# Latent attention rebuilt, the norm between two models folded in, and another order in a softmax loop

## The reference

```
return rms_norm(h, g_final)                         # end of the first model, x of the second

cq, ckv, kr = split(x @ w_in, [384, 640])           # latent attention
q = heads(rms_norm(cq, q_norm) @ w_uq)              # 16 heads, 64 plain + 32 rotary columns
kv = heads(rms_norm(ckv, kv_norm) @ w_ukv)          # 64 key + 64 value columns each
logits = (qn @ kn.T + rotary(qr) @ rotary(kr).T) * 96 ** -0.5
p = softmax(where(kpos <= qpos, logits, -1e30))
out = from_heads(p @ v) @ w_o
```

## Time and profile before

| what | value |
|---|---|
| median of three runs | 2787.2 us |
| the profiled execution | 2785.38 us, span 2783.6 us |
| mean granted clock of TensorE | 0.975 |
| PE busy | 2654.8 us (95%) |
| VectorE busy | 1745.5 us (63%) |
| ScalarE busy | 1342.4 us (48%) |
| HBM read | 452.38 MB, 163 GB/s over the span |

### The profile page before, as it was taken

One profiled execution on the slowest core, in us unless ns is written; L12 is line 12 of the kernel. 1 busy time (PEld: TensorE's weight loads), 2 busy tenths in 40 slices (PEclk: granted clock), 3 DMA queues, 4 the chain that ended last, 5 costly groups with the idle time before them and its releaser, 6 DMA issues.

```text
span 2783.6 us, 38348 instructions
## 1 busy us (share of the span) xinstructions
PE 2654.8 (95%) x14970; PEld 2271.9 (82%) x14970; DVE 1745.5 (63%) x1901; ACT 1342.4 (48%) x1554; POOL 6.8 (0%) x17
## 2 busy tenths in 40 slices
PE   7899998999899999999999999999789999999998
PEld 7688786887788988888887888887668888888887
DVE  6666676666666656666666666666536666666665
ACT  5444454444544545454444544544435454454543
POOL 0000000000000000000000000000000000000000
PEclk9899997999999999999999999999879999999999
DMA  7255442554455335555533455554305555543452
GB/s 281 76 184 182 174 167 76 184 182 173 158 187 194 139 106 201 191 176 189 194 139 119 168 195 181 182 191 156 114 31 197 182 180 187 190 162 124 170 184 73
DMA packets 63479, 454.95 MB, mean 163 GB/s; under 512 B 7104, under 2 KB 7360, under 8 KB 8848
## 3 DMA queue, kind: packets, MB, share of 16 engines
q1 hardware_dynamic: 61920, 448.82, 45.3%
q0 software_dynamic: 1024, 3.51, 0.4%
q10 hardware_dynamic: 432, 1.13, 0.1%
HBM read 452.38 MB, written 1.05 MB: 163 GB/s over the span
## 4 chain that ended last, share of the span: by engine, by line
PE 86%; DVE 6%; ACT 5%; issue 2%; DMA 1%; SPq 0%; DVEq 0%; ACTq 0%
PE tb L450 23%; PE tb L448 13%; PE acc L258 9%; PE acc L260 9%; PE acc L259 9%; PE tb L447 3%; ACT w_hi L200 2%; DVE w_lo L207 2%; PE acc L227 2%; PE acc L229 1%; PE acc L230 1%; PE tb L289 1%; PE acc L771 1%; PE acc L773 1%; PE acc L772 1%
## 5 line engine op out<-in xcount | busy, mean ns | idle before, releaser
L207 DVE TENSOR_TENSOR w_lo<-raw,w_hi 128x2048 fp32r<-128x2048 f32 x426 | 975.1, 2291 | 376.6 <-ACT w_hi L200 375.7
L200 ACT ACTIVATE w_hi<-raw 128x2048 fp32r<-128x2048 f32 x426 | 814.3, 1912 | 368.2 <-PE acc L260 303.8
L450 PE MATMUL tb<-xT,w_hi 128*128 128x512 f32 x2772 | 988.3, 396 | 0.0
L448 PE MATMUL tb<-xT,w_lo 128*128 128x256 f32 x3168 | 819.1, 279 | 0.0
L448 PEld LDWEIGHTS tb<-xT,w_lo 128*128 128x128 f32 x3168 | 597.2, 189 | 33.8
L450 PEld LDWEIGHTS tb<-xT,w_hi 128*128 128x128 f32 x2772 | 521.2, 188 | 106.7
L258 PE MATMUL acc<-w_hi,cat 128*128 128x512 f32 x1024 | 403.1, 394 | 6.7 <-issue 3.5
L260 PE MATMUL acc<-w_lo,cat 128*128 128x512 f32 x1024 | 400.0, 391 | 0.0
L259 PE MATMUL acc<-w_hi,cat 128*128 128x512 f32 x1024 | 399.9, 391 | 0.0
L258 PEld LDWEIGHTS acc<-w_hi,cat 128*128 128x128 f32 x1024 | 193.0, 189 | 46.7 <-issue 4.0
L260 PEld LDWEIGHTS acc<-w_lo,cat 128*128 128x128 f32 x1024 | 192.8, 188 | 40.8
(11 more groups left out here) (309 smaller groups left out, 3340.4 us busy)
## 6 DMA issues: line engine op xcount, KB each, us to landing
raw<-in_stream SPq DMA_DIRECT2D x426, 1024.0 KB, 4.8
h<-in_x SPq DMA_DIRECT2D x2, 512.0 KB, 5.1
gain<-in_gains POOLq DMA_DIRECT2D x2, 512.0 KB, 9.3
xn<-in_gates POOLq DMA_DIRECT2D x2, 512.0 KB, 8.7
out<-xn SPq DMA_DIRECT2D x2, 512.0 KB, 2.7
cst<-in_consts ACTq DMA_DIRECT2D x1, 960.5 KB, 12.5
big<-in_pT POOLq DMA_DIRECT2D x2, 256.0 KB, 3.0
gain<-in_gains POOLq DMA_DIRECT2D x1, 320.0 KB, 3.8
```

The costliest lines, as they stand in the source:

```text
L200: act.activation(w_hi[:, k % SPLIT, :], raw[:, k % RAW, :], ACT.Copy).then_inc(hi_done, 1)
L207: dve.tensor_tensor(w_lo[:, k % SPLIT, :], raw[:, k % RAW, :], w_hi[:, k % SPLIT, :], ALU.subtract).then_inc(lo_done, 1)
L448: last = pe.matmul(banks[f][:, 0:SEQ], lo, xT[:, kt, 0, :], start=False, stop=False)
L450: last = pe.matmul(banks[f], hi, both, start=False, stop=kt == KT - 1)
```

## The change

Three edits.

The norm between the models has no stage of its own. `gain_T` of the first swiglu is multiplied with `g_final` once at the start (VectorE), so TensorE can transpose h at once, with its lower half ahead of the last `ple` product (`following`). GpSimd writes h times gain to `xn`; ScalarE squares h and `xn`, VectorE finds the first factor, from it and the second sum the second factor, and their product. The spread comes one `up` product later in that stage, and VectorE scales `xn` into h for the residual behind the first `hidden_lo`.

In the softmax loop the transposes of pair p-1 stand directly behind the scores of pair p, ahead of all feed, and ScalarE copies the transposed weights of p-1 ahead of the exponentials of p; its splits come behind both.

The latent stage is rebuilt. The input product has the latents on the partitions (`columns`), kv first, then q with the rotary key in the chunk's free columns. Sums of squares are taken on TensorE (a product with a constant column). Only kv is scaled by its factor; q's factor goes into the cosine and sine tables and so applies to the rotary columns and, with a cosine of 1 there, to the plain ones. Nothing is transposed. K and V have their own columns in the weights. Products run as units: seven ahead of the loop (`LAT_FIRST`), the others as its feed (`LAT_STEPS`), in three banks of `acc`. GpSimd copies the rotary key to the heads in two halves, where VectorE did it in one. The chunk order in the stream follows the units.

```diff
-    out.append(("bridge", 0, c, n)); n += 1
+    n += 1
...
+        def following(n):
+            return n + 2 if n + 1 == BRIDGE else n + 1
...
+                to = xn[:, t, :] if n != BRIDGE + 1 else cut(4096 + D * t, D)
+                act.activation(to, h[:, t, :], ACT.Square, accum_out=ss[:, t:t + 1]).then_inc(*sig("sumsq", (n, t)))
+            if n == BRIDGE + 1:
+                for t in range(TT):
+                    act.wait_ge(*when("gained", t))
+                    act.activation(cut(4096 + D * (2 + t), D), xn[:, t, :], ACT.Square,
+                                   accum_out=ss2[:, t:t + 1]).then_inc(*sig("sumsq", (BRIDGE, t)))
+                act.wait_ge(*when("meansq", BRIDGE))
+                act.activation(rms, ms, ACT.Sqrt).then_inc(*sig("root", BRIDGE))
...
+            if n == BRIDGE + 1:
+                for t in range(TT):
+                    dve.wait_ge(*when("sumsq", (n, t)))
+                dve.tensor_scalar(ms, ss, 1.0 / D, EPS, ALU.mult, ALU.add).then_inc(*sig("meansq", BRIDGE))
+                newton(dve, rms, ms, r0, r1, first_rstd, BRIDGE)
+                dve.tensor_tensor(r2, first_rstd, first_rstd, ALU.mult).then_inc(*sig("own", "bridge0"))
+                for t in range(TT):
+                    dve.wait_ge(*when("sumsq", (BRIDGE, t)))
+                dve.wait_ge(*when("own", "bridge0"))
+                dve.tensor_tensor(ss2, ss2, r2, ALU.mult).then_inc(*sig("own", "bridge1"))
+                dve.wait_ge(*when("own", "bridge1"))
+                dve.tensor_scalar(ms, ss2, 1.0 / D, EPS, ALU.mult, ALU.add).then_inc(*sig("meansq", n))
+                newton(dve, rms, ms, r0, r1, rstd, n)
+                dve.tensor_tensor(rstd, rstd, first_rstd, ALU.mult).then_inc(*sig("own", "bridge2"))
+                dve.wait_ge(*when("own", "bridge2"))
...
-            spread(pe, n, acc[:, 3, 0:SEQ])
+            if n != BRIDGE + 1:
+                spread(pe, n, acc[:, 3, 0:SEQ])
...
+                    if n == BRIDGE + 1 and first and j == 0:
+                        spread(pe, n, acc[:, 3, 0:SEQ])
...
+            if n == BRIDGE + 1:
+                for t in range(TT):
+                    dve.tensor_scalar(h[:, t, :], xn[:, t, :], first_rstd[:, t:t + 1], None, ALU.mult)
...
-                feed.some(p, 0)
...
+                feed.some(p, 0)
                 feed.some(p, 1)
                 if p >= 1:
...
-                if p < N_PAIRS:
-                    act.wait_ge(*when("top", (i, p)))
...
-                behind(p, 0)
...
-                behind(p, 1)
-                behind(p, 2)
+                if p < N_PAIRS:
+                    act.wait_ge(*when("top", (i, p)))
+                    for u in range(2):
+                        hd, dst = 2 * p + u, probs[:, 2 * (p % 2) + u, :]
+                        act.activation(dst[:, 0:P], tb[:, u, 0:P], ACT.Exp, bias=nmx[:, hd, 0:1], scale=scale,
+                                       accum_out=sm[:, hd, 0:1])
+                        last = act.activation(dst[:, P:CAUSAL], tb[:, u, P:CAUSAL], ACT.Exp, bias=nmx[:, hd, 1:2],
+                                              scale=scale, accum_out=sm[:, hd, 1:2])
+                    last.then_inc(*sig("exps", (i, p)))
+                for part in range(3):
+                    behind(p, part)
...
+        IN_KV, IN_Q, UP_Q, UP_KV, W_O = (0,), (1, 2), (4, 5, 7), (3, 6), 8
...
+        LAT_FIRST = [("k", 0, 0), ("k", 0, 1), ("v", 0, 0), ("v", 0, 1), ("q", 0), ("q", 1), ("rot", 0)]
...
+        LAT_STEPS = [
+            [[("rot", 1)], [("q", 2)], [("q", 3)]],
+            [[("rot", 2)], [("q", 4)], [("q", 5)]],
+            [[("rot", 3)], [("k", 1, 0)], [("k", 1, 1)]],
+            [[("rot", 4)], [("v", 1, 0)], [("v", 1, 1)]],
+            [[("rot", 5)], [("q", 6)], [("q", 7)]],
+            [[("rot", 6)], [("block", k) for k in (0, 1, 2, 3)], [("rot", 7)]],
+            [[("block", 4), ("block", 5)], [("block", 6), ("block", 7)], []],
+            [[("block", 8), ("block", 9)], [("block", 10), ("block", 11)], [("block", 12)]],
+            [[("block", 13), ("block", 14)], [("block", 15)], [("block", 16), ("block", 17)]]]
...
+            def q(self, unit, p):
+                pe, i = self.pe, self.i
+                g, h0 = q_of_pair[p]
+                k = self.c + UP_Q[g]
+                pe.wait_ge(lo_done, k + 1)
+                if p == 0:
+                    pe.wait_ge(*when("q_lo", (i, 1)))
+                s, width = k % SPLIT, MLA_Q_GROUPS[g] * MLA_HD
+                for u in range(2):
+                    o = lat_bank(unit)[R, u * SEQ:(u + 1) * SEQ]
+                    for kt in range(3):
+                        a = kt * width + (h0 + u) * MLA_HD
+                        hi, lo = w_hi[:, s, a:a + MLA_HD], w_lo[:, s, a:a + MLA_HD]
+                        pe.matmul(o, hi, q_T[:, kt, 0, :], start=kt == 0, stop=False)
+                        pe.matmul(o, hi, q_T[:, kt, 1, :], start=False, stop=False)
+                        last = pe.matmul(o, lo, q_T[:, kt, 0, :], start=False, stop=kt == 2)
...
+            def rot(self, unit, p):
+                self.pe.wait_ge(*when("pair_taken", (self.i, p)))
+                self.pe.matmul(lat_bank(unit)[R, :], rotl[R, 0:MLA_HD],
+                               m_q[R, 2 * p:2 * p + 2, :].rearrange("p a t -> p (a t)"),
+                               start=True, stop=True).then_inc(*sig("rotated", (self.i, p)))
...
+                    if t == 1:
+                        split_hi(act, c, UP_KV[g] + SPLIT)
...
+        def lat_turn(dve, i, p):
+            b, r = m_q[R, 2 * p:2 * p + 2, :], two(m_turn[R, :])
+            dve.wait_ge(*when("rotated", (i, p)))
+            if p:
+                dve.wait_ge(*when("turned", (i, p - 1)))
+            dve.tensor_tensor(r, two(lat_bank(("rot", p))[R, :]), sin_q[R, :].unsqueeze(1).to_broadcast([MLA_HD, 2, SEQ]), ALU.mult)
+            dve.tensor_tensor(b, b, cos_q[R, :].unsqueeze(1).to_broadcast([MLA_HD, 2, SEQ]),
+                              ALU.mult).then_inc(*sig("own", ("turn", i, p)))
+            dve.wait_ge(*when("own", ("turn", i, p)))
+            dve.tensor_tensor(b, b, r, ALU.add).then_inc(*sig("turned", (i, p)))
...
+        def lat_sum(pe, i, k, tiles):
+            pe.wait_ge(*when("lat_sq", (i, 2 * k)))
+            for t in range(TT):
+                for j, sq in enumerate(tiles):
+                    last = pe.matmul(tb[:, k, t:t + 1], sq[:, t * P:(t + 1) * P], every[:, 0:1], start=j == 0,
+                                     stop=j == len(tiles) - 1)
...
+            columns(pe, c, lambda f: acc[:, 2, f * SEQ:(f + 1) * SEQ], 2, KT, SEQ, after=x_ready(pe, n))
+            for u, _ in enumerate(columns_by_steps(pe, c + 1, lambda f: acc[:, 0, f * SEQ:(f + 1) * SEQ], 2, KT, SEQ)):
+                if u == 6:
+                    lat_sum(pe, i, 0, [sq_kv[:, 0:SEQ], sq_kv[:, SEQ:2 * SEQ]])
+                if u == 8:
                     spread(pe, n)
-            for j, (at_, m) in enumerate(LAT_T):
-                if j in (0, 3):
-                    pe.wait_ge(*when("lat_normed", (i, j // 3)))
+            for u, _ in enumerate(columns_by_steps(pe, c + 2, lambda f: acc[:, 1, f * SEQ:(f + 1) * SEQ], 2, KT, SEQ)):
+                if u == 1:
+                    lat_spread(pe, i, 0)
+                if u == 8:
+                    pe.wait_ge(*when("rb", n))
+                    pe.wait_ge(*when("kr_in", i))
+                    pe.matmul(tb[R, 3, 0:SEQ], rotl[R, 0:MLA_HD], kr_buf[R, :], start=True, stop=True).then_inc(*sig("kr_rot", i))
+            feed = LatFeed(pe, i, c)
+            feed.run(LAT_FIRST[0:1])
+            lat_sum(pe, i, 1, [sq_q[:, j * SEQ:(j + 1) * SEQ] for j in range(3)])
+            feed.run(LAT_FIRST[1:5])
+            lat_spread(pe, i, 1)
+            feed.run(LAT_FIRST[5:])
...
+            used(act, c)
+            act.activation(sq_kv, acc[:, 2, :], ACT.Square).then_inc(*sig("lat_sq", (i, 0)))
+            split_hi(act, c, SPLIT)
+            spread_act(act, n, "mla")
+            root(0)
+            act.wait_ge(*when("lat_spread", (i, 0)))
+            act.activation(kv_rb, tb[:, 2, 0:SEQ], ACT.Copy).then_inc(*sig("kv_rb", i))
+            act.wait_ge(*when("kr_in", i))
+            q_hi(0, acc[:, 0, 0:SEQ])
+            act.activation(sq_q[:, 0:SEQ], acc[:, 0, 0:SEQ], ACT.Square).then_inc(*sig("lat_sq", (i, 1)))
+            act.wait_ge(*when("kv_s", i))
+            for j in range(2):
+                act.activation(kv_T[:, j, 0, :], kv_s[:, j * SEQ:(j + 1) * SEQ], ACT.Copy,
+                               scale=gain_T[:, N_NORMS, j:j + 1]).then_inc(*sig("kv_hi", (i, j)))
+            split_hi(act, c, 1 + SPLIT)
+            used(act, c + 2)
+            for j in range(2):
+                q_hi(1 + j, acc[:, 1, j * SEQ:(j + 1) * SEQ])
+            act.activation(sq_q[:, SEQ:3 * SEQ], acc[:, 1, :], ACT.Square).then_inc(*sig("lat_sq", (i, 2)))
+            lat_act(act, i, c, LAT_FIRST[0:1])
+            root(1)
```

(48 more changed lines are left out.)

457 lines of the change are left out of this document (219 added, 238 removed).

## The result

The changed kernel takes 2741.8 us (median of four runs, 2735.3 to 2747.3) against 2787.4 beside it; the ratio is 0.983, its 95% interval 0.9815 to 0.9845. The forecast was 2735, 6.8 us too low, inside its range. The profiled execution took 2742.9 around a span of 2741.1, so it is 42.5 us under the profiled 2785.4 of before, where the sum of the prediction had 52.

What follows compares the result with a forecast made beforehand. TensorE, busy 95% of the span, was taken as the limit, with idle and slow-clock places from latency chains. Gains 42+8+2-0.2=52 took 2785.4 to 2733.4, on the median 2735; range 2716 to 2760.

Steps and rivals of the forecast that it cites:

- Part 1: Between the halves, without a separate norm phase: first weight product 7.1 us sooner, clock about 1.4; gain 8 (4 to 9).
- The cover of the late factor: Second half's first stage: three up products of about 5.6 us each run before the spread at about 731, factor ready near 729.
- Part 2: Latent stage, front: first scores at 1958.1 where they start at 2001.9 today, after a gap of 2.6 us.
- Part 3: Latent softmax loop: 69.3 us with 9.8 of PE gaps, clock loss 4; gain 42 (36 to 50) together with the front.
- Part 4: `moba` loop: PE's 3.94 us idle at step 6 shrinks, pair 7's scores begin 2.1 earlier; gain 2 (0 to 4).
- Start: Kernel start: the extra product and the removed memset, 0.2 us lost.
- A: Latent stage: VectorE's gaps mostly absent, PE work alone counts; gain 67, 2720 us; chance 0.14.
- B: Latent loop: the clock stays at 0.50, 15 to 20 us more; gain 34, 2753 us; chance 0.14.
- C: GpSimd holds VectorE: first latent scores 2 to 9 us later, up to 3 between the halves; 2742 us; chance 0.15.
- D: Latent stage: clock at 1.2 GHz from its first gap to its end, kernel 13 us slower, 2800; chance 0.03.
- E: Rebuilt order only moves latency, each new wait as long as the old; near 2777 us; chance 0.04.
- The forecast case: Whole kernel, likeliest case: gain 52 us, bounds 40 to 69, hence 2718 to 2747; chance 0.50.

Runs made afterwards that it cites:

- late splits: Changed kernel with VectorE's latent-loop weight splits one step later and the head sums' split ahead of the feed: 2729.1 us, ratio 0.9787.

## Why the prediction was right, and the terms that were off

**Part 1**, 8 forecast, 7.0 measured, and the same stretch of 226.5 in seven profiles. The first weight product came at 717.99, or 6.8 us sooner once the 3.8 of late start is taken off (7.1 forecast). The clock gave back next to nothing, not 1.4: the wait of 1.91 was followed by 3.4 us at the low clock. GpSimd's share was taken as 0 and is 1.3. The cover of the late factor held.

**Part 2**, first scores 43.8 us sooner forecast, 42.4 measured. Counted from the stage's first flip, the input product was to end at 22.9 and ended at 23.5; the seven units with sums and spread were to take 12.0 and took 12.9. The term that stands out is the ten sums of squares: taken as 0.1, they hold TensorE for 0.91 and 1.36 us, and the 1.3 for the later six with the spread was 1.60. The bound I gave, 0.14 each, was too low for all ten (0.23). The other 0.6 are the units, each a little longer than forecast. The gap behind them was 2.52, forecast 2.6.

**Part 3**, 73.3 us from first scores to last value product forecast with the clock, 77.3 measured. The gaps are 0.31, 2.58, 1.89, 2.44 and 1.89, sum 9.1 against 9.8, the four large ones each behind a split as forecast. The mis-sized term is the clock: 4 taken, about 7 found (half of 13.9 us at 0.50; late splits took away 10.5 us of that and gained 5.0 by it). My interval for it, 0 to 9.5, held both. It rested on 4 us at 0.50 behind a gap, of which the earlier trace rows show only 2; the traces have 3.4 behind such a gap, and 6.8 in two places of single runs. TensorE's own work is then 61, forecast 60.3. The forecast's 69.3 is 0.8 under the sum of its own terms, 60.3 and 9.8; the prediction gives no reason for that.

**Part 4**, 2 forecast, 2.2 and 2.1 measured, with a wait of 2.5 before the scores.

**Start**, 0.2 lost forecast, 4.1 measured: not an effect of the changed start, since the same start also took 139.8; what it is an effect of stays open. By the medians the gain is 45.5 against 52. That the time fell 6.8 us from the forecast has this clock in it, which no term foresaw.

**Rivals.** A fell: the gaps are there. B fell: 0.91, not 0.5, in the loop. C had VectorE held for 1.6 us, past the 1.3 from which I said it decides, and a VectorE instruction longer than 2.29 us was one of my signs of being wrong; yet it cost only 0.4 there, and 1.3 between the halves through the clock. The slack of 1.3 was underrated. So C was right in its mechanism and is a part of why the gain came out low. D and E fell. The forecast case came in near the low end of its bounds: 42.5, or 46 without the loss at the start, where they were 40 to 69.

## What to carry to other kernels

An in-order engine that serves both a latency chain and bulk work should take the bulk one step late, behind the chain's last instruction: 8.9 us of waits cost 13.9 here, because stretches at the low clock stood behind them. Forecast the order of instructions behind each wait, since moving a neighbour (the head sums) only moved the wait. Give GpSimd's arithmetic the moments when VectorE idles, or start it behind a VectorE instruction, so that GpSimd is the one that waits, and price it by what PE has to do meanwhile, not by how long VectorE is held.

## What the runs showed of the hardware

- One stage with the same waits of 2.0, 2.0 and 3.3 us took 139.2 to 143.3 us in 13 profiles, by where among them the granted clock goes to 0.50.
- The length of a wait alone did not decide whether 0.50 follows. Between the halves a wait of 1.91 was followed by it in all eight profiles that have it, and one of 1.55 in neither of two; but the wait of 2.84 ahead of them was followed by it in one profile of eleven, and one of 2.15 in the `moba` stage in ten of thirteen.
- An f32 matmul of one column, 128 by 128 weights, takes 0.23 us of TensorE, nearly what a 512-column matmul of the weights took (0.228).
- GpSimd beside VectorE: a product of 128x1024 takes 2.4 us. A 32x2048 copy takes 1.88 when it is first and 3.89 to 3.96 when a 2.29 us split is ahead of it; the split took 3.90 when the copy was first, and a two-column operation 0.90 for 0.17.
